# Norm sums and head means in a two-block transformer kernel: one float32 product replaced by a split on VectorE and two rounded products

## The reference

```python
def rmsnorm(x, g):                      # over the width of 1024: the norm sums
    y = x32 * lax.rsqrt(jnp.mean(jnp.square(x32), axis=-1, keepdims=True) + EPS)

o = rmsnorm(o, norm_g) * jax.nn.silu(...)      # HGRN2: over each head's 64 values
def head_group_norm(y):                        # retention: over each head's 64 values
    mu = jnp.mean(yf, axis=-1, keepdims=True)
    var = jnp.mean(jnp.square(yf - mu), axis=-1, keepdims=True)
    return (yf - mu) * lax.rsqrt(var + GN_EPS)
```

## Time and profile before

| what | us |
|---|---|
| median of 3 runs | 2325.79 |
| lowest and highest run | 2325.03, 2326.75 |
| span of the profiled execution | 2323.9 |
| TensorE busy in it | 2298.8 |
| VectorE, ScalarE, GpSimd busy | 1090.5, 857.0, 1180.2 |

### The profile page before, as it was taken

One profiled execution on the slowest core, in us unless ns is written; L12 is line 12 of the kernel. 1 busy time (PEld: TensorE's weight loads), 2 busy tenths in 40 slices (PEclk: granted clock), 3 DMA queues, 4 the chain that ended last, 5 costly groups with the idle time before them and its releaser, 6 DMA issues.

```text
span 2323.9 us, 34938 instructions
## 1 busy us (share of the span) xinstructions
PE 2298.8 (99%) x11446; PEld 1833.9 (79%) x11446; DVE 1090.5 (47%) x1866; ACT 857.0 (37%) x1313; POOL 1180.2 (51%) x1554
## 2 busy tenths in 40 slices
PE   8999999999999999999999999999999999999998
PEld 6777777778888888877788888888777788888886
DVE  5468865444312314536755243354346755242444
ACT  4354454454322224323343222245333343222254
POOL 5346653345555455544345555456534256556563
PEclk9999999999999999999999999999999999999999
DMA  4221121124223222333323323223333222323232
GB/s 168 86 91 51 56 64 64 55 86 130 91 100 109 81 99 91 104 135 100 100 67 106 103 88 108 82 86 109 104 127 91 83 91 99 109 90 104 84 93 82
DMA packets 66859, 218.90 MB, mean 94 GB/s; under 512 B 8241, under 2 KB 8625, under 8 KB 66753
## 3 DMA queue, kind: packets, MB, share of 16 engines
q1 hardware_dynamic: 57888, 196.87, 25.4%
q10 hardware_dynamic: 8864, 20.62, 2.8%
HBM read 211.14 MB, written 2.13 MB: 92 GB/s over the span
## 4 chain that ended last, share of the span: by engine, by line
issue 43%; POOL 39%; PE 14%; DVE 2%; POOLq 1%; ACT 1%; DMA 1%; DVEq 0%; ACTq 0%; SPq 0%
POOL w_lo L2051 38%; PE acc L306 4%; PE acc L308 4%; PE acc L307 4%; POOLq L2098 1%; PE sc L508 1%; PE po L459 0%; PE po L643 0%; PE sc L643 0%; POOLq L2047 0%; DMA raw<-in_w_ple_gate 0%; DMA x<-in_x 0%; POOLq L2059 0%; DVE x_queries L1624 0%; PE po L551 0%
## 5 line engine op out<-in xcount | busy, mean ns | idle before, releaser
L2051 POOL TENSOR_TENSOR w_lo<-raw,w_hi 128x256 fp32r<-128x256 f32 x1486 | 1132.1, 794 | 1076.2 <-ACT w_hi L845 1072.7
L306 PE MATMUL acc<-act_hi,w_hi 128*128 128x512 f32 x1696 | 673.9, 397 | 9.0 <-DVE act_lo L1385 8.0
L308 PE MATMUL acc<-act_hi,w_lo 128*128 128x512 f32 x1696 | 662.5, 391 | 0.0
L307 PE MATMUL acc<-act_lo,w_hi 128*128 128x512 f32 x1696 | 661.9, 390 | 0.0
L845 ACT CAST w_hi<-raw 128x1024 fp32r<-128x1024 f32 (+1 forms) x388 | 390.7, 1017 | 401.5 <-PE acc L308 230.4
L306 PE MATMUL acc<-y_hi,w_hi 128*128 128x512 f32 x1068 | 422.0, 395 | 0.0
L308 PE MATMUL acc<-y_hi,w_lo 128*128 128x512 f32 x1068 | 416.3, 390 | 0.0
L307 PE MATMUL acc<-y_lo,w_hi 128*128 128x512 f32 x1068 | 416.0, 390 | 0.0
L306 PEld LDWEIGHTS acc<-act_hi,w_hi 128*128 128x128 f32 x1696 | 319.4, 188 | 79.2 <-issue 9.6
L308 PEld LDWEIGHTS acc<-act_hi,w_lo 128*128 128x128 f32 x1696 | 319.2, 188 | 67.5
L307 PEld LDWEIGHTS acc<-act_lo,w_hi 128*128 128x128 f32 x1696 | 319.7, 188 | 65.6 <-issue 1.9
(11 more groups left out here) (336 smaller groups left out, 2174.5 us busy)
## 6 DMA issues: line engine op xcount, KB each, us to landing
raw<-in_w_ffn_wide SPq DMA_DIRECT2D x120, 512.0 KB, 3.2
raw<-in_w_in SPq DMA_DIRECT2D x102, 512.0 KB, 3.2
raw<-in_w_rest SPq DMA_DIRECT2D x72, 512.0 KB, 3.2
raw<-in_w_gate SPq DMA_DIRECT2D x24, 512.0 KB, 3.2
raw<-in_w_ple_gate SPq DMA_DIRECT2D x16, 512.0 KB, 3.2
raw<-in_w_branch SPq DMA_DIRECT2D x24, 256.0 KB, 2.6
raw<-in_w_ffn_narrow SPq DMA_DIRECT2D x16, 384.0 KB, 3.0
swap<-wab ACTq DMA_DIRECT2D x64, 64.0 KB, 2.0
```

The source lines that it names most:

```text
L306: nc.tensor.matmul(dst, w[0], src[0], start=start, stop=False)
L307: nc.tensor.matmul(dst, w[0], src[1], start=False, stop=False)
L308: return nc.tensor.matmul(dst, w[1], src[0], start=False, stop=stop)
L2051: last = nc.gpsimd.tensor_tensor(w_lo[:, slot, cut], raw[:, slot % 2, cut], w_hi[:, slot, cut], ALU.subtract)
```

## The change

VectorE copies each total or square into a rounded tile (`two_parts`: a cast, a drain, and a subtraction that leaves the rest), and TensorE multiplies both with rounded constants and adds them up in the bank. The constants are rounded once at the start by ScalarE (two more copies of 128x128); an unused constant is dropped. The norms 1 to 7 (eight sums) and the twelve head means change; norm 0, the final norm and the latent sums don't. In HGRN2's stage the splits stand on VectorE between the two latent panels; in the retention's stage each stands ahead of the pair's multiplication with the gate, and twelve products of the output projection (`fox(1, range(4))`) are moved ahead of the last pair's mean.

```diff
             def norm(r):
                 pe.wait_ge(S("norm_total"), r + 1)
-                last = nc.tensor.matmul(sc[:, 0, :], c["ones"], probs[:, 0, :], start=True, stop=True)
-                if r == 2:
-                    last = nc.tensor.matmul(sc[:, 1, :], c["ones"], probs[:, 1, :], start=True, stop=True)
+                if r == 0:
+                    last = nc.tensor.matmul(sc[:, 0, :], c["ones"], probs[:, 0, :], start=True, stop=True)
+                else:
+                    for i, parts in enumerate((sum_parts, mid_parts) if r == 2 else (sum_parts,)):
+                        for half in range(2):
+                            last = nc.tensor.matmul(sc[:, i, :], consts_r[:, 2, :], parts[:, half, :],
+                                                    start=half == 0, stop=half == 1)
                 last.then_inc(S("norm_sum"), 1)
...
-            def head_mean(ready, count, done, p, src, bank=mean_bank):
+            def head_mean(ready, count, done, p, parts, bank=mean_bank):
                 pe.wait_ge(S(ready), count)
-                nc.tensor.matmul(bank[p], c["head_mean"], src, start=True, stop=True).then_inc(S(done), 1)
+                for half in range(2):
+                    last = nc.tensor.matmul(bank[p], consts_r[:, 3, :], parts[half], start=half == 0, stop=half == 1)
+                last.then_inc(S(done), 1)
...
                 for p in range(PAIRS):
-                    head_mean("r_sq", l * 4 + (p + 1), "r_var", p, square_r(p), ret_bank)
-                for j in range(1, 4):
+                    if p == PAIRS - 1:
+                        fox(1, range(4))
+                    head_mean("r_parts", l * 4 + (p + 1), "r_var", p, mean_parts_r(p), ret_bank)
+                for j in range(2, 4):
                     fox(j, range(4))
...
+            nc.scalar.copy(consts_r[:, 2, :], c["ones"]).then_inc(S("mask_rounded"), 1)
+            nc.scalar.copy(consts_r[:, 3, :], c["head_mean"]).then_inc(S("mask_rounded"), 1)
...
-            def norm_end():
+            def two_parts(total, high_part, low_part):
+                v.tensor_copy(high_part, total)
+                dve.drain()
+                return v.tensor_tensor(low_part, total, high_part, ALU.subtract)
+
+            def norm_end(r):
+                dve.drain()
+                if r:
+                    two_parts(probs[:, 0, :], sum_parts[:, 0, :], sum_parts[:, 1, :])
+                if r == 2:
+                    two_parts(probs[:, 1, :], mid_parts[:, 0, :], mid_parts[:, 1, :])
                 dve.drain().then_inc(S("norm_total"), 1)
...
             evacuate(0, N_C, 1, lambda i: wv[:, 0, :], "c_raw")
+            for p in range(PAIRS):
+                dve.wait_ge(S("b_sq"), p + 1)
+                two_parts(b_stat[p], *mean_parts_b(p)).then_inc(S("b_parts"), 1)
             evacuate(0, N_C + 1, 1, lambda i: wv[:, 1, :], "c_raw")
...
                     dve.wait_ge(S("r_sq"), l * 4 + (p + 1))
+                    two_parts(square_r(p), *mean_parts_r(p)).then_inc(S("r_parts"), 1)
                     v.tensor_tensor(wb[:, p + 4, :], wb[:, p + 4, :], wa[:, p, :], ALU.mult)
```

More of the change, by code:

```diff
@@ L56 @@
 SEGMENTS2 = ["in2", "ffn_wide", "ffn_narrow", "ple_a", "ple_b", "ple_gate"]
-CONSTS = ["ident", "anti", "ones", "head_mean", "mask", "rope"]
+CONSTS = ["ident", "ones", "head_mean", "mask", "rope"]
 N_MASKS = 7
@@ L101, in build @@
     masks = sb("masks", [P, N_MASKS, P // 2])
-    consts_r = sb("consts_r", [P, 3, P], F32R)
+    consts_r = sb("consts_r", [P, 4, P], F32R)
     params = sb("params", [P, N_PARAMS])
@@ L115, in build @@
     positions = alias("positions", "vcur", [P, T], I32)
+    sum_parts = alias("sum_parts", "probs_t", [P, 2, T], F32R)
+    mid_parts = alias("mid_parts", "tab", [P, 2, T], F32R)
     tail = 8 * T * 4
@@ L167, in square_r, with mean_parts_b, mean_parts_r @@
         return wb[:, (p + 1) % PAIRS, :]
+    def mean_parts_b(p):
+        return y_hi[:, p + 4, :], merged_hi[:, p, :]
+    def mean_parts_r(p):
+        return y_hi[:, p + 4, :], y_lo[:, p + 4, :]
     def value_tile_r(l, p):
@@ L651, in _ @@
             gemm(0, N_C, 2, KD, act_in)
+            pe.wait_ge(S("mask_rounded"), 4)
             for p in range(PAIRS):
-                head_mean("b_sq", p + 1, "b_mean", p, b_stat[p])
+                head_mean("b_parts", p + 1, "b_mean", p, mean_parts_b(p))
             def latent_sum(first, count):
@@ L1368, in add_to_x @@
                 if normed:
-                    norm_end()
+                    norm_end(normed[0])
             def low_of_tile(name, k, src, hi, lo):
@@ L2028, in _ @@
                 if l + 1 < LAYERS:
-                    norm_end()
+                    norm_end(l * 3 + 5)
             dve.wait_ge(S("norm_rstd"), 9)
@@ L2124, in constant_arrays @@
     k, q = i[:, None], i[None, :]
-    table = {"ident": k == q, "anti": k + q == P - 1, "ones": np.ones((P, P)), "head_mean": (k // HD == q // HD) / HD}
+    table = {"ident": k == q, "ones": np.ones((P, P)), "head_mean": (k // HD == q // HD) / HD}
     mask1 = np.where(q // CHUNK <= k // CHUNK, 0.0, MASKED)
```

4 lines of the change are left out of this document (2 added, 2 removed).

## The result

The changed kernel takes 2328.12 us in the median of 20 runs (2326.38 to 2330.09), the kernel before 2325.19 in 20 runs beside them (2324.29 to 2326.75): a ratio of 1.0013 with the interval [1.0007, 1.0019]. I had forecast 0.6 us faster; it is 2.9 us slower. That is still less than the 0.2% that I called no change, but the ratio's interval leaves out 1, and it lies on the other side.

The account below looks back on a forecast made before the run. TensorE, busy 2298.8 of 2323.9 us, was taken as the bound. Terms summed as 2.05 - 0.67 - 0.75 - 1.1 + 1.1 = 0.6 us faster, giving 2325.2 us, range 2321.0 to 2328.6.

Parts of the forecast that it names:

- product saves: Each of 20 changed products: two rounded products at 0.45 us replace one float32 product at 0.87, saving 0.41 us.
- norms 1, 3, 6: Splits covered by panels before TensorE needs the total; 0.41 us saved at each, within 2.05 for five norms.
- norms 4, 7: Counted with norms 1, 3 and 6 as covered by panels: 0.41 us saved at each, no loss.
- norm 5: After the side input's gates, cover 0.7 us: split beside GpSimd stalls TensorE 1.08 us, net loss 0.67.
- norm 2: Two splits delay GpSimd's panels and so a load ScalarE awaits: loss of 0.75 us, bounds 0 and 1.7.
- HGRN2's end: Four splits delay the second latent fetch by 2.4 us, ScalarE's idle 1.03 absorbs part: loss of 1.1 us.
- retention, two layers: GpSimd idle, a 1.1 us stall at the third mean: 0.55 us gained per layer, 1.1 for two.
- The other four: Norms 3, 4, 6 and 7, said to have at least norm 1's 7.3 us of cover against 1.3 to 2.1.
- D: Rival: splits queue behind GpSimd at HGRN2's end, upper prices at norms 2 and 5; 2.2 us slower, 2328.0; chance 0.16.
- B: Rival: splits run clear of GpSimd or slip in between; 4.05 us faster, 2321.7; chance 0.20.
- C: Rival: the full saving is kept, as waits are shorter than slack at some later point; 2317.6 us; chance 0.06.
- E: Rival: a pair of rounded products takes as long as one float32 product (0.87 us); 3.0 us slower, 2328.8; chance 0.06.

Follow-up runs that it names:

- changed again: The changed kernel run and profiled once more, unaltered, against the kernel before: median 2328.12 us against 2325.30, ratio 1.0011.
- run with the norms only: Changed kernel with HGRN2 and retention head means back to one float32 product, only the norms split: 2326.35 us against 2325.30 before, ratio 1.0005.
- run with float32 products: Only HGRN2's four splits kept, their results unused, TensorE taking float32 products behind them; all else float32: 2327.34 us against 2325.20 before, ratio 1.0008.
- run with ScalarE's squares: Only HGRN2's means split, ScalarE writing the rounded square by a second squaring, VectorE only subtracting: 2324.82 us against 2325.20 before, ratio 0.9996.
- HGRN2 only: Changed kernel with norms and retention back to float32, only HGRN2's four head means split: 2327.99 us against 2325.30 before, ratio 1.0011.
- retention only: Changed kernel with norms and HGRN2 back to float32, retention's eight head means split, twelve products still moved: 2325.49 us against 2325.30 before, ratio 1.0001.

## Why the prediction was wrong, point by point

The single terms, prediction against ledger (changed again, the usual execution; plus is a loss):

| term | predicted | measured |
|---|---|---|
| product saves | 0.41 | 0.41 to 0.45 |
| norms 1, 3, 6 | -1.23 | -1.31 |
| norms 4, 7 | -0.82 | +0.23 |
| norm 5 | +0.67 | +0.77 |
| norm 2 | +0.75 | +0.58 |
| HGRN2's end | +1.1 | +1.42, and +0.19 behind it |
| retention, two layers | -1.1 | -1.07 |
| transposes at 1734 | 0 | +0.67 |
| final norm's parts | 0 | +0.58 |
| sum | -0.6 | +2.1 |

**The step that failed** is "The other four have at least as much [cover] ... Cover: those panels." It asked only whether the total is ready before TensorE wants it, and at these five norms it was. It did not ask what the split, covered itself, does to GpSimd, though I had done exactly that sum at norm 2, where I charged the split with a later load. At norms 4 and 7 the side input's gate panel is on GpSimd at the moment of the split, and its load, ScalarE's queue and the accumulator banks hang on it. That is 1.06 us in the usual execution (0.55 + 0.51) and 2.45 in the one that was profiled first. It is the largest part of the 2.7 us between the two sums and not the whole of it: without it the sum would still be +1.0.

The splits of norms 1, 3 and 6 ran beside GpSimd too (in the run with the norms only, casts of 0.94 to 0.95 us and subtractions of 1.06 to 1.07), and at norm 1 the next load was issued just as late, by 0.63 us, yet TensorE lost nothing. The traces show the difference: in the kernel before, ScalarE's next rounding waits for TensorE there, and at norm 4 for the load itself. Norm 1, then norm 4:

```profile
604.15 1.05 ACT L845 CAST w_hi<-raw 128x1024 fp32r<-128x1024 f32 x1 [4.96 <-PE acc L308]
...
1578.93 1.05 ACT L845 CAST w_hi<-raw 128x1024 fp32r<-128x1024 f32 x1 [0.84 <-DMA raw<-in_w_ple_gate]
```

At norm 1 the load had landed 0.58 us before the rounding, so a load that is 0.63 late is just in time. At norms 3 and 6 ScalarE waits 6.14 us for TensorE, at norm 7, as at norm 4, for the load.

**HGRN2's end** was right in mechanism. The fetch came 2.6 us late (2.4 forecast), VectorE's stretch started 1.1 late on before's clock, and TensorE lost 1.35 instead of 1.1, since the stretch itself took 0.26 longer, by one more meeting with GpSimd as I read it. The run with float32 products shows that what TensorE saves there is worth nothing while the fetch is late, as written in the prediction, and the run with ScalarE's squares gives the bound that I had named for a clear fetch, 1.1 (measured 1.29).

**Norm 5, norm 2 and the retention** are within 0.2 us. The waits in the rows count from the recorded end of the product before, which overlaps the next one's start by 0.16 us; from start to start, as the prediction reckons, TensorE stalls for 1.02 us at norm 5 (1.08 forecast) and 0.94 at the third mean (1.1 forecast). The wait at 970.75 is 1.67 for the 1 to 2 forecast, and the load behind norm 2 was issued 0.78 later (0.75 forecast). The net gain of a layer (0.5) is the one forecast although the stall is shorter: the first product of such a group takes 0.34 us to the next (1169.02 - 1168.68) and not 0.227. `r_y` caused no stall.

**The 0.67 at 1734** was in no part of the sum. There VectorE scales the forgetting attention's weights (L1495) and TensorE transposes them. Up to that point VectorE and GpSimd keep the same distances to 0.02 us in before and after, and then one instruction starts 0.35 us later and takes 0.33 longer. Changed kernel, then before:

```profile
1735.76 0.17 DVE L1493 RECIPROCAL cols<-cols 128x1 f32<-128x1 f32 x1
1736.36 0.84 DVE L1495 TENSOR_SCALAR probs<-probs,cols 128x128 f32<-128x128 f32 x1 [0.44 <-issue]
```

```profile
1732.60 0.16 DVE L1463 RECIPROCAL cols<-cols 128x1 f32<-128x1 f32 x1
1732.85 0.51 DVE L1465 TENSOR_SCALAR probs<-probs,cols 128x128 f32<-128x128 f32 x1
```

It happened in both profiles of the changed kernel there, and in three of the others (HGRN2 only, its float32 variant, retention only) at 1796 instead, in the float32 variant at 1113 as well. It happened in neither profile of before and not in the other six. I read it as a turn at the shared port that is missed and costs one GpSimd instruction. What decides it isn't shown: at 1734 GpSimd's instruction starts 0.05 us ahead of the reciprocal in profiles with the step and in those without.

**The final norm's 0.58** has two parts. 0.36 come at 2313.34, only in the two profiles of the changed kernel, where a multiplication on VectorE (L2050) starts 0.62 us after the one before and not 0.23 (L2016 of before); why stays open. The rest, 0.22 here and 0.44 to 0.48 in five other profiles, is TensorE's clock. In the first profile of the changed kernel the granted clock fell from 1.00 to 0.50 (the level of 1.2 GHz) at 2316.20, ahead of TensorE's last product at 2316.73; in before it fell at 2315.99, and the product at 2313.34 was through. Between that product and the one before it TensorE had waited 0.73 us for ScalarE (0.32 in before). Changed kernel, then before:

```profile
2316.73 2.08 PE L847 MATMUL sc<-probs,consts 128*128 128x512 f32 x2 [0.73 <-ACT probs L1321]
```

```profile
2313.34 1.13 PE L830 MATMUL sc<-probs,consts 128*128 128x512 f32 x2 [0.32 <-ACT probs L1302]
```

ScalarE takes up the result 2.12 us after the product's start and not 1.17. So the lower clock costs 0.95 us, of which the ledger, which ends at the product's second record, shows 0.48. In the usual execution it costs 0.68. Why the clock falls ahead of that product in some of the kernels and behind it in others isn't known.

The baseline hid a part of the miss: the three runs at hand had a median of 2325.79, twenty have 2325.19. From the latter the same forecast would have been 2324.6, so the error in the change itself is 3.5 us (-0.6 against +2.9), and in time it shows as 2.9.

Of the rivals, D was nearest in time (2328.0) and wrong in mechanism: its upper prices at norm 2, norm 5 and HGRN2 were not reached. B, C and E failed by the ledger. That the stated range held 2328.12 is luck: it was wide enough for D, and what filled it were terms that the sum had as gains or at nothing.

**The price of a meeting** was read too neatly. One's own time plus the other's would be 0.69 + 0.71 = 1.40 us for a subtraction, and not the 1.2 that the prediction says agrees with it. The prices that it took from the rows (0.89, 1.2 and 2.05 for a split) held all the same: the splits at HGRN2's end start 2.0 us apart.

## What to carry to other kernels

An instruction that is covered by its own deadline can still cost, when it shares a port with an engine that is off the critical path: follow that engine's delay through the buffer it frees, the load that waits for it and the queue behind that load. Place such work in the other engine's gaps, or give it to the third engine, and the same edit gains where it lost. And when a change has many small places, compare the starts of the same instructions in both traces place by place: medians of 11 runs cannot separate half a microsecond here. The ledger can, to 0.1 or 0.2, where a step comes again in a second profile; it sees nothing ahead of its first place and behind its last.
